# A two-part transformer on one Trainium2 core: context stream prepared one stage early, low-rank norms applied at eviction

## What is computed

```python
x = rms_norm(h, norm_final)                       # end of the first block
mod   = silu(c)     @ ada_w[0] + ada_b[0]         # shift sh1, scale sc1, ...
mod_c = silu(c_ctx) @ ada_w[0] + ada_b[0]         # csh1, csc1, ...
h  = x   * (1 + sc1)  + sh1
hc = ctx * (1 + csc1) + csh1                      # needs nothing of the first block
# mla, for h and hc alike
q  = (_rms_norm(t @ w_dq, q_norm) @ w_uq)         # 1024 -> 512 -> 8 x (128 + 64)
c_kv, k_pe = split(t @ w_dkv)                     # 1024 -> 256 + 64
kv = _rms_norm(c_kv, kv_norm) @ w_ukv             # 256 -> 8 x (128 + 128)
# _rms_norm(x, g) = x * rsqrt(mean(x*x) + eps) * g, one factor for each token
```

## Time and profile before

| | |
|---|---|
| median of 3 runs | 2428.21 us (2427.79 to 2428.53) |
| the profiled execution's own time | 2428.19 us |
| its span (first to last instruction) | 2426.4 us |
| TensorE busy | 2307.8 us (95%) |
| DVE busy | 1693.0 us (70%) |
| ACT busy | 1081.8 us (45%) |
| DMA | 374.75 MB, mean 154 GB/s |
| TensorE's mean granted clock | 0.974 of full |

### The profile page before, as it was taken

The page is one execution under the profiler, slowest core; times in us unless marked ns, Lnnn a source line. Parts: engine busy times, 40 slices in busy tenths (PEclk is TensorE's granted clock), DMA queues, the critical chain, the costliest instruction groups (busy, mean ns, idle before and its releaser), DMA issues.

```text
span 2426.4 us, 39847 instructions
## 1 busy us (share of the span) xinstructions
PE 2307.8 (95%) x16368; PEld 2095.0 (86%) x16368; DVE 1693.0 (70%) x3234; ACT 1081.8 (45%) x1918; POOL 0.2 (0%) x4
## 2 busy tenths in 40 slices
PE   7999999999999999999999899988999998998998
PEld 7869999899999999986999766577888877968997
DVE  6678875688777887667887544458777865367667
ACT  4385444564444544447644333434122225264433
POOL 0000000000000000000000000000000000000000
PEclk9899999999999999989999899998999999999999
DMA  6405765356655566640576422022554423323553
GB/s 220 143 23 199 249 207 187 122 177 246 220 191 184 203 235 214 208 144 22 200 252 208 152 84 70 1 78 99 170 174 158 155 92 108 101 91 105 183 182 122
DMA packets 71092, 374.75 MB, mean 154 GB/s; under 512 B 7424, under 2 KB 17664, under 8 KB 38912
## 3 DMA queue, kind: packets, MB, share of 16 engines
q1 hardware_dynamic: 61456, 361.52, 43.6%
q10 hardware_dynamic: 9456, 10.68, 1.5%
HBM read 369.03 MB, written 1.05 MB: 153 GB/s over the span
## 4 chain that ended last, share of the span: by engine, by line
PE 81%; DVE 11%; ACT 4%; DMA 2%; issue 1%; ACTq 0%; DVEq 0%
PE ps L412 76%; DVE w_lo L1324 4%; PE ps L660 2%; DMA w_raw<-weights 2%; PE ps L643 2%; ACT w_hi L907 2%; DVE ps L1358 1%; PE ps L600 1%; DVE hid_f L1601 1%; ACT p_ring L1021 1%; PE ps L589 1%; DVE hid_f L1623 1%; DVE a_lo L1324 1%; ACT a_hi L943 0%; DVE p_ring L1871 0%
## 5 line engine op out<-in xcount | busy, mean ns | idle before, releaser
L412 PE MATMUL ps<-a_hi,w_hi 128*128 128x256 f32 (+1 forms) x3008 | 911.8, 303 | 54.4 <-DVE w_lo L1324 21.8
L412 PE MATMUL ps<-a_lo,w_hi 128*128 128x256 f32 (+1 forms) x3008 | 903.9, 300 | 0.0
L412 PE MATMUL ps<-a_hi,w_lo 128*128 128x256 f32 (+1 forms) x3008 | 903.5, 300 | 0.0
L1324 DVE TENSOR_TENSOR w_lo<-w_raw,w_hi 128x1024 fp32r<-128x1024 f32 (+1 forms) x632 | 698.8, 1147 | 198.1 <-ACT w_hi L907 197.7
L907 ACT CAST w_hi<-w_raw 128x1024 fp32r<-128x1024 f32 (+1 forms) x632 | 593.3, 987 | 501.2 <-DMA w_raw<-weights 500.2
L412 PEld LDWEIGHTS ps<-a_hi,w_hi 128*128 128x128 f32 x3008 | 579.5, 193 | 83.3 <-issue 46.1
L412 PEld LDWEIGHTS ps<-a_lo,w_hi 128*128 128x128 f32 x3008 | 579.7, 193 | 18.2 <-issue 0.5
L412 PEld LDWEIGHTS ps<-a_hi,w_lo 128*128 128x128 f32 x3008 | 579.5, 193 | 18.3
L412 PE MATMUL ps<-hid_hi,w_hi 128*128 128x256 f32 (+1 forms) x1364 | 424.8, 311 | 5.9 <-DVE w_lo L1324 2.0
L412 PE MATMUL ps<-hid_lo,w_hi 128*128 128x256 f32 (+1 forms) x1364 | 422.1, 309 | 0.0
L412 PE MATMUL ps<-hid_hi,w_lo 128*128 128x256 f32 (+1 forms) x1364 | 422.1, 309 | 0.0
(11 more groups left out here) (180 smaller groups left out, 2038.2 us busy)
## 6 DMA issues: line engine op xcount, KB each, us to landing
w_raw<-weights SPq DMA_DIRECT2D x250, 1024.0 KB, 4.8
pe_sb<-weights SPq DMA_DIRECT2D x96, 512.0 KB, 5.6
w_raw<-weights SPq DMA_DIRECT2D x64, 704.0 KB, 4.0
pe_sb<-na_bias ACTq DMA_DIRECT2D x32, 128.0 KB, 2.1
qk<-qk ACTq DMA_DIRECT2D x8, 256.0 KB, 7.1
X<-x_t SPq DMA_DIRECT2D x1, 1024.0 KB, 7.5
X<-c_rows ACTq DMA_DIRECT2D x2, 512.0 KB, 4.5
X<-ctx_t ACTq DMA_DIRECT2D x1, 1024.0 KB, 8.0
```

The source lines that it names most:

```text
L412: return nc.tensor.matmul(out, stationary, moving, start=start, stop=stop)
L1324: return v.tensor_tensor(out, a, b.bitcast(F32), ALU.subtract)
```

## The change

1. **Context stream.** At the start of ffn 3 ACT's queue loads the context into `ctx_raw`, a part of the q buffer that is free there. DVE finishes the first 16 modulation vectors after that ffn's `norm_row`. Each of the eight `down` steps of ffn 3 gets a context tile: ACT scales and shifts it (256 columns), ACT makes the high part, DVE the low part.
2. **End of the first network.** `residual_sums` and `residual_spread` of ffn 3 move into the first mla unit (`norm_at`). `run_enter` copies the row factor, splits mla unit 2, and makes the operand of the other stream alone: DVE multiplies by gain and factor, ACT scales and shifts, ACT high, DVE low. The scaling of the residual by ALPHA follows, in 16 instructions of 256 columns instead of eight of 512.
3. **First three mla units by stream.** `by_stream` runs the three units over the context columns first and then over the other 256, with rings "AA", "DD", "EE" (a new ring E, banks 4 and 5). The weights of all three stay in their slots until the second pass.
4. **Norm factors at eviction.** The compressed rows go to the next products with their gain but without the token factor: ACT copies the high part from PSUM and squares, DVE makes the low part and adds the squares. `low_sums` (four matmuls with one column each) and `low_spread` (four of 128 columns) give the token factors. DVE multiplies the q, rotary, key and value products by the factor as it evicts them; ACT no longer evicts these.

```diff
@@ TensorE
-                if i == 3:
-                    residual_sums()
-                    residual_spread()
+            def by_stream(rings, hook):
+                units = [unit(cnt, r) for r in rings]
+                for c in (CTX, LAT):
+                    xs = parts(a_hi, a_lo, c)
+                    operands()
+                    for first, (u, made) in zip([True, False, False], units):
+                        if c == CTX:
+                            begin(u)
+                            for j, (_, p, _) in enumerate(made):
+                                start_product(rings[units.index((u, made))][j], p)
+                        order = [(k, j) for k in range(KD) for j in range(2)] if first else [(k, j) for j in range(2) for k in range(KD)]
+                        for k, j in order:
+                            if first and j == 0:
+                                operand_at(k)
+                            bank, p, (ready, _) = made[j]
+                            last = fm_tile(ps[:, bank, c], u % SLOTS, j * KD + k, xs[k], k == 0, k == KD - 1)
+                            if c == LAT and k == KD - 1:
+                                last.then_inc(ready, 1)
+                            if c == CTX and first and j == 1:
+                                hook(k)
@@ def run_mla (TensorE)
-                for _ in range(2):
-                    fm_unit("AA", a)
-                fm_unit("AA", a)
-                sum_squares(QR, 2 * S)
-                fm_unit("AD", a)
-                sum_squares(KR, 2 * S)
+                by_stream(["AA", "DD", "EE"], norm_at)
+                low_sums(0)
+                fm_unit("AD", parts(a_hi, a_lo, ALL))
+                low_spread(0)
+                low_sums(1)
                 operands(QR)
                 cq = parts(cq_hi, cq_lo, ALL)
+                fm_unit("AAAA", cq)
+                low_spread(1)
                 for _ in range(2):
                     fm_unit("AAAA", cq)
-                fm_unit("AAAA", cq)
@@ def run_ffn (ACT)
+                if i == 3:
+                    act.dma_start(ctx_raw, ctx_t.rearrange("(k p) t -> p k t", p=P)).then_inc(ctx_loaded, 16)
...
                     residual_tile(made, made[1] - d0, gain)
+                    if i == 3:
+                        context_tile(made[1] - d0)
+                def context_tile(k):
+                    if k == 0:
+                        act.wait_ge(ctx_loaded, 16)
+                        act.wait_ge(mods_ready, 1)
+                    wait(act, operand, n["tile"] - 1)
+                    nc.scalar.activation(norm_slot[k % 2], ctx_raw[:, k, :], ACT.Identity, bias=mods(0, 0, k, 1), scale=mods(0, 1, k, 1)
+                                         ).then_inc(normed, 1)
+                    high_tile(a_hi[:, k, CTX], norm_slot[k % 2])
@@ def run_mla (ACT)
+                def low_tiles(made, ring, dst, gain):
                     for m in range(2):
...
+                        nc.scalar.activation(dst[:, m, :], ps[:, bank, :], ACT.Copy, scale=gain[:, m:m + 1]).then_inc(norm_hi, 1)
...
+                        nc.scalar.activation(t_ring[:, n["low"] % 2, :], ps[:, bank, :], ACT.Square).then_inc(low["squared"], 1)
@@ def run_ffn (DVE)
                 norm_row()
+                if i == 3:
+                    finish_mods(0, 2 * KD)
+                    sync()
+                    scale_mods(0, 1, mods_ready)
...
                     add_square()
                     if k == KD - 1:
                         ahead(u1)
+                    if i == 3:
+                        n["tile"] += 1
+                        dve.wait_ge(norm_hi, n["tile"])
+                        minus(a_lo[:, k, CTX], norm_slot[k % 2], a_hi[:, k, CTX]).then_inc(operand, 1)
@@ def run_enter (DVE)
+                norm_row()
+                split(cnt.n["unit"] + 2)
+                for k in range(KD + 1):
+                    if k < KD:
+                        v.scalar_tensor_tensor(X[:, k, LAT], X[:, k, LAT], col("norm_final", k), r_row[:, :], ALU.mult, ALU.mult
+                                               ).then_inc(x_norm, 1)
@@ def run_mla (DVE)
+                u, made = next_unit("AA")
+                low_tiles(0, made, "A", cq_hi[:, 0:2, :], cq_lo[:, 0:2, :], col("q_norm", 0, 2))
+                u, made = next_unit("DD")
+                ahead(u)
+                low_tiles(0, made, "D", cq_hi[:, 2:4, :], cq_lo[:, 2:4, :], col("q_norm", 2, 2))
...
+                u, made = next_unit("A" * 8)
+                for h in range(MLA_H):
+                    bank = ready(made[h])
+                    v.tensor_tensor(k_sb[:, h, :], ps[:, bank, :], low_row[1], ALU.mult).then_inc(taken["A"], 1)
+                ahead(u)
```

## The result

The changed kernel takes 2414.47 us (median of 4 runs, 2412.6 to 2417.32), the kernel before beside it 2428.37 (4 runs, 2427.79 to 2433.26): a ratio of 0.9939, 95% interval 0.9922 to 0.9957. It is faster, and the median lies in the predicted range, 0.5 us under its upper end. The profiled execution took 2412.60 us, with a span of 2410.8 and a granted clock of 0.976 (before: 2428.19, 2426.4 and 0.974).

What follows compares the result with a forecast made beforehand. TensorE set the end for 81% of the chain and DVE for 11%, so gains lie where TensorE waits or runs slowly. Ten terms sum to -19.05, from 2428.2 to 2409.2 us; 8-in-10 range 2404 to 2415.

Steps and rivals of the forecast that it cites:

- (a): Entry and first three mla units: 47.4 us become 35.6 with six 256-column passes at full clock, a gain of 11.8.
- (b): Norm of the compressed q: a gap and slow restart of 8.5 us become four one-column sums, a gain of 7.5.
- (c): Norm of kv: 2.7 us of gap and 0.4 of restart become a spread and four sums, a gain of 1.5.
- (e): First q product: TensorE's 1.28 us wait for ACT's eviction goes, with 0.1 of restart, a gain of 1.4.
- (f): Key products: DVE evicts them behind w_lo, so a new wait of 1.3 us, with the restart 1.4 lost.
- (g): Value products: the 1.9 us wait for DVE's eviction shrinks to 1.0, a gain of 0.9.
- (h): Down steps of ffn 3: context tiles delay the weight split in three steps, 1.8 us lost, bounds 0.6 to 4.
- (i): Start of ffn 3: two small DVE instructions and their waits lose 0.35 us; the context load costs nothing.
- (j): Seventh down step of ffn 3: the 1 MB context load leaves it, a gain of 0.3 us.
- rival of a late stream: Second mla pass: other stream's operand late; 10 us late brings back 8, 2417 us; late or several rivals, chance 0.04.
- DVE did not inherit the stall: Rival: DVE, evicting everything and making every w_lo, delays norm of q, down steps and keys: 2416 us, chance 0.18.
- The stalls were not already paid: Rival: down steps lose only 0.6, keys' wait is 0.5, hooks 0.4 each: 2406 us, chance 0.22.

Runs made afterwards that it cites:

- factors_alone: The kernel before with only the norms' token factors applied at eviction, context load and whole-width units as before: median 2417.37 us, ratio 0.9950, stretch 318.45.
- early_split: The changed kernel with DVE's w_lo of the units two ahead made in halves, in idle gaps between evictions: median 2409.05 us, ratio 0.9905, stretch 307.07.
- after_again: The changed kernel run once more, nothing edited: median 2412.83 us, ratio 0.9919, stretch 309.94.

## Why the prediction was right, point by point

Measured in the two profiled executions, against its terms:

| term | predicted | measured |
|---|---|---|
| (a) entry and three units | -11.8 | -11.2 |
| (b) norm of q | -7.5 | -7.6 |
| (c) norm of kv | -1.5 | -1.3 |
| (d) second spread | +0.8 | +0.9 |
| (e) wait for ACT's q eviction | -1.4 | -1.55 |
| (f) keys | +1.4 | +1.5 |
| (g) values | -0.9 | -0.9 |
| (h) down steps | +1.8 | +2.95 |
| (i) start of ffn 3 | +0.35 | +0.3 |
| (j) seventh down step | -0.3 | -0.5 |
| sum in the stretch | -19.05 | -17.5 |
| outside it | 0 | +1.9 |

**The entry (a)** held as a mechanism: no gap over 0.5 us, clock 1.00, six passes at the step of 0.120. The context tiles were ready, and the second stream never waited: DVE's low parts of its first and last tile have the rows

```profile
1372.19 0.42 DVE L1365 TENSOR_TENSOR a_lo<-p_ring,a_hi 128x256 fp32r<-128x256 f32 x1 [0.71 <-ACT a_hi L960]
...
1378.93 0.42 DVE L1365 TENSOR_TENSOR a_lo<-p_ring,a_hi 128x256 fp32r<-128x256 f32 x1 [0.52 <-ACT a_hi L960]
```

TensorE's second pass starts after the 144 context matmuls and the two hooks, with

```profile
1379.90 0.28 PE L416 MATMUL ps<-a_hi,w_hi 128*128 128x256 f32 x1
```

The first tile (ready at 1372.61) was there 7.3 us ahead of its use, where 8 were said. The last (ready at 1379.35) is needed seven k steps, 42 matmuls of 0.120 us, into the pass, near 1384.9, so it had 5.6 us to spare. The prediction's 1.3 us "at the last tile" is the distance to the start of the pass, not to the tile's use, which its own rival puts at 1379.9 in the time of before: by its own numbers the cover was 6.4. Measured like the 1.3 it is 0.55: DVE began the stream 9.6 us behind the last ffn matmul, as said, but the first tile took 2.0 us through three engines and the others came 0.96 apart, not 0.9. By these rows a stream 10 us late would bring back some 4.4 us (10 less 5.6, an estimate), so that the rival of a late stream would end near 2414 and not at 2417.

The term's 0.6 us too much are 0.3 for a wait that I had not listed, before the fourth matmul (1361.24 to 1361.65: the second half of unit 0's w_lo, whose load landed at 1358.13, after 4.86 us), its restart of 0.1, and the two hooks, which with their restarts cost 1.0 in place of 0.7.

The cut of 512 columns into twice 256 was paid as the rows said. Each pass kept to 0.120 us a step, so that 144 pairs cost 1.9 us over whole steps of 0.227. By what the Trainium skill has in "TensorE: Matmul & The Clock Gate" (Back-to-back issue gap), N/2.4 + 2.5 ns for a lone matmul, it would have been 0.4. No pass of six came near that. A lone matmul is not this stream, where each comes with a weight load of its own; that the weight loads set the difference is not shown by any run here.

**The norms (b), (c), (d)** came within 0.2 each. The sums after the third unit had no wait at all before them, where 0.2 was allowed and up to 3 feared: unit 3's split on ACT was in time. Since factors_alone gives -9.0 for (b) to (g) from the kernel before, where the terms add up to -9.1, this part is shown on its own.

**The evictions (e), (f), (g)** came within 0.15: 1.20 us at the third key product and 0.99 at the third value product, where 1.3 and 1.0 were said. early_split shows that their cause is the one named, w_lo queued in one piece ahead of the eviction: moved, both went.

**The down steps (h)** are the term that was mis-sized: +1.8 said, +2.95 measured, still under its upper bound of 4. The step was to be 8.73 us for three steps; the adds are 8.93 apart:

```profile
1302.82 0.42 DVE L1934 TENSOR_TENSOR X<-ps,X 128x256 f32<-128x256 f32 x1 [1.25 <-PE ps L416]
1311.75 0.42 DVE L1934 TENSOR_TENSOR X<-ps,X 128x256 f32<-128x256 f32 x1
1320.67 0.41 DVE L1934 TENSOR_TENSOR X<-ps,X 128x256 f32<-128x256 f32 x1
1329.60 0.41 DVE L1934 TENSOR_TENSOR X<-ps,X 128x256 f32<-128x256 f32 x1
```

I had priced the context tile's scale and shift at 0.42, the duration of the square of the same shape. It takes 0.59 on ACT (the second line; the square stands above it, the fourth is the split that it delays):

```profile
1312.20 0.42 ACT L969 ACTIVATE t_ring<-X 128x256 f32<-128x256 f32 x1 [3.99 <-DVE X L1934]
1312.53 0.59 ACT L1228 ACTIVATE p_ring<-qk,mod 128x256 f32<-128x256 f32 x1
1313.14 0.41 ACT L960 CAST a_hi<-p_ring 128x256 fp32r<-128x256 f32 x1
1313.46 2.82 ACT L937 CAST w_hi<-w_raw 128x768 fp32r<-128x768 f32 x4
```

That is 0.17 us for each of three steps, 0.5 of the 1.15 missing. The rest, 0.65, was missing from the start. TensorE shows it, here in the second of the three:

```profile
1319.27 0.28 PE L416 MATMUL ps<-hid_hi,w_lo 128*128 128x256 f32 x1
1320.08 0.39 PE L416 MATMUL ps<-hid_hi,w_hi 128*128 128x256 f32 x1 [0.53 <-DVE w_lo L1365]
1320.30 0.28 PE L416 MATMUL ps<-hid_lo,w_hi 128*128 128x256 f32 x1
...
1324.01 0.28 PE L416 MATMUL ps<-hid_hi,w_lo 128*128 128x256 f32 x1
1324.25 0.39 PE L416 MATMUL ps<-hid_hi,w_hi 128*128 128x256 f32 x1
1324.48 0.28 PE L416 MATMUL ps<-hid_lo,w_hi 128*128 128x256 f32 x1
```

Beyond the step of 0.12 it loses 0.69 before the unit's first half, 0.12 before its second, and 0.10 to 0.11 in the matmul that restarts behind each: 1.0 in all, and the same in the third step (the first lost 0.94). The sum's base was too small for this. It took ffn 2's loss as 0.6, the two waits of 0.3 that the waits view lists; in steps of TensorE each of them costs 0.43, and 0.10 for the restart. But ffn 2's fifth residual add, like its first, comes as soon as TensorE is done, and so tells what the four steps between them cost:

```profile
966.29 0.42 DVE L1919 TENSOR_TENSOR X<-ps,X 128x256 f32<-128x256 f32 x1 [1.56 <-PE ps L412]
```

From 933.34 that is 32.95 us, where four steps of 7.92 are 31.7: ffn 2 loses 1.3, with a third wait of 0.13 and its restart that the view leaves out. With 1.3 for 0.6 and the 0.5 of the scale and shift the term would have been 3.0, which is what was measured. The prediction's own step of 8.73 pointed there too: three of them are 2.4 over 7.92 each, not 1.8. The lower bound, "ffn 2 as it is", was likewise 1.3 and not 0.6, so the rival in which the down steps lose only 0.6 had no row behind it.

**The start (i) and the load (j)** were right: from the reciprocal to the first residual add the change costs 0.3, and the 1 MB context load beside the split units costs nothing that can be seen (ACT waits for no weight load there, and from 21 us behind the reciprocal on, at 1188.97 and 1190.92, it is 111.90 us to that add in both kernels). Its absence at the seventh down step gave 0.5.

**The rivals.** DVE did not inherit the stall; of its three conditions, one was met in part (the down steps, 1.15 of the 2.2 reckoned). The stalls were not already paid either. The clock never fell behind the new waits. The time of the profiled execution, 2412.60, lies 3.4 us over the sum of 2409.2: 1.15 from (h), 0.6 from (a), offset by small terms to 1.6, and 1.9 from outside the stretch, 1.45 of it in nsa 1, which was taken as constant. The range was made from the unknown costs of the change alone, with no width for a stage outside it that moves by 3.7 us between executions; so it held the median of 2414.47 by only 0.5 us, and that it did is in part luck. (after_again's median, 2412.83, lies 2.2 us inside.)

## What to carry to other kernels

When a norm's factor keeps TensorE waiting, give it the columns that do not need the factor first and apply per-token factors at eviction: here the order was worth 9.8 us and the deferred factors 9.0, while preparing operands earlier had no worth of its own, only as what the order needs. Then look at every in-order queue that took over the work and ask what each new instruction stands in front of: putting the context tile behind the weight split and cutting the split into halves that fit the idle gaps gave 6.1 us more without removing any work. Read the effect in the stretch of the change, cut at events that both kernels have, as other stages vary by more than the term in question.

## What the runs showed of the hardware

- On ACT a scale and shift with a per-partition bias and scale took 0.59 to 0.60 us for 128x256, the square and the cast of the same shape 0.42 and 0.41: the same shape is no price for another function's operands.
- The granted clock in nsa 1 differs between executions of one kernel (0.71 and 0.67 over the same 40 us), and with it the stage's time, by 3.6 us. In the runs of before shown here the whole kernel ranges from 2425.64 to 2435.37.
- Matmuls that only keep TensorE occupied kept its clock at full through 11 us of waiting, and gave back 2.5 us; the entry itself became no longer by them (11.49 us, 11.99 before). The waits remain, so real work from another place was worth about four times as much in the same idle time (9.8).
